# Last head of the latent attention: query weights in four free places, gates of its own, latent queries and a page turn between its products, rotary chunk first; scores of tile 4 as 320 + 320

## What is computed

```python
q = jnp.einsum('bsc,chd->bshd', cq, w_qb)
q_nope, q_rope = q[..., :QK_NOPE], q[..., QK_NOPE:]
...
k_nope = jnp.einsum('bsc,chn->bshn', ckv, w_uk)
v = jnp.einsum('bsc,chv->bshv', ckv, w_uv)
...
sc = (jnp.einsum('bqhn,bkhn->bhqk', qn_b, k_nope)
      + jnp.einsum('bqhr,bkr->bhqk', qr_b, kpe)).astype(jnp.float32) * MLA_SCALE
sc = jnp.where(kpos[None, :] <= qpos[:, None], sc, NEG_INF)
p = jax.nn.softmax(sc, axis=-1).astype(v.dtype)
return jnp.einsum('bhqk,bkhv->bqhv', p, v)
...
# samples: the query goes into the latent, and the paged latents are keys and values
q_lat = jnp.einsum('bthn,chn->bthc', q_nope, w_uk)
s_past = (jnp.einsum('bthc,bsc->bhts', q_lat, past_ckv)
          + jnp.einsum('bthr,bsr->bhts', q_rope, past_kpe)).astype(jnp.float32) * MLA_SCALE
...
h <- h + RMSNorm_post( W_o( attn(RMSNorm_pre(h)) * silu(gate) ) )
```

## Time and profile before

| | us |
|---|---|
| median of 3 runs | 1676.52 |
| the profiled execution, its time | 1678.97 |
| its span, first to last instruction | 1677.3 |
| busy: TensorE matmul / weight load | 1583.8 / 1484.5 |
| busy: VectorE / ScalarE / GpSimd | 825.3 / 547.3 / 736.8 |
| mean granted TensorE clock | 0.987 |

### The profile page before, as it was taken

How to read it: one execution, slowest core, us unless ns; L and a number is a source line. 1 busy time by engine, 2 the same in 40 slices (tenths; PEclk the granted TensorE clock), 3 DMA queues, 4 the chain that set the end, 5 groups by cost and what they waited for, 6 DMA issues and landing times.

```text
span 1677.3 us, 28038 instructions
## 1 busy us (share of the span) xinstructions
PE 1583.8 (94%) x10778; PEld 1484.5 (89%) x10778; DVE 825.3 (49%) x1459; ACT 547.3 (33%) x1203; POOL 736.8 (44%) x891
## 2 busy tenths in 40 slices
PE   7999999899999999999998888999899999988997
PEld 7999999799999898999997557999799999966796
DVE  5137311676675757575665430006873421178426
ACT  4113101344444444444443320012231311277322
POOL 2432323154655545455545512546522324278720
PEclk9999999999999999999999999999999999999998
DMA  4112232021111211112117977227254323354223
GB/s 179 60 52 100 85 123 99 19 63 55 64 57 56 70 55 60 48 61 66 64 39 257 330 284 271 64 75 239 99 216 151 106 76 132 102 154 121 76 79 149
DMA packets 101406, 186.92 MB, mean 111 GB/s; under 512 B 11058, under 2 KB 65091, under 8 KB 100995
## 3 DMA queue, kind: packets, MB, share of 16 engines
q1 hardware_dynamic: 86628, 139.36, 24.9%
q0 software_dynamic: 8448, 24.65, 4.2%
q10 hardware_dynamic: 6208, 21.26, 3.2%
HBM read 137.42 MB, written 49.89 MB: 112 GB/s over the span
## 4 chain that ended last, share of the span: by engine, by line
PE 80%; DVE 8%; ACT 5%; issue 3%; DMA 2%; POOL 1%; SPq 1%; DVEq 0%; ACTq 0%; POOLq 0%
PE ps L128 26%; PE ps L928 8%; PE ps L2123 6%; PE ps L994 6%; PE ps L2331 5%; PE ps L978 4%; ACT s_prob L2603 3%; PE ps L934 3%; PE ps L941 2%; PE ps L958 2%; PE ps L959 2%; PE ps L962 2%; PE ps L960 2%; PE ps L961 2%; PE ps L2257 2%
## 5 line engine op out<-in xcount | busy, mean ns | idle before, releaser
L654 POOL TENSOR_SCALAR b_prob<-b_prob,b_share 128x896 f32<-128x896 f32 (+7 forms) x128 | 97.4, 762 | 194.5 <-DVE b_share L856 192.6
L1779 POOL CAST w_hi_d<-w_raw_d 128x1024 fp32r<-128x1024 f32 x38 | 42.3, 1113 | 225.0 <-PE ps L128 109.4
L128 PE MATMUL ps<-a_xh,w_hi_a 128*128 128x344 f32 x552 | 119.5, 325 | 11.0 <-DVE a_xl L397 11.0
L755 ACT ACTIVATE b_pth<-ps 128x512 fp32r<-128x512 f32 (+1 forms) x160 | 86.2, 554 | 104.9 <-PE ps L978 95.4
L128 PE MATMUL ps<-a_xl,w_hi_a 128*128 128x344 f32 x552 | 118.4, 323 | 0.0
L128 PE MATMUL ps<-a_xh,w_lo_a 128*128 128x344 f32 x552 | 118.1, 323 | 0.0
L746 ACT ACTIVATE b_prob<-ps,b_least 128x896 f32<-128x896 f32 (+7 forms) x128 | 94.8, 743 | 58.1 <-DVE b_least L847 57.1
L847 DVE TENSOR_REDUCE b_least<-ps 128x1 f32<-128x896 f32 (+7 forms) x128 | 96.1, 751 | 33.3 <-PE ps L964 32.5
L861 DVE TENSOR_TENSOR b_ptl<-ps,b_pth 128x512 fp32r<-128x512 f32 (+1 forms) x160 | 99.0, 631 | 27.0 <-ACT b_pth L755 26.0
L128 PEld LDWEIGHTS ps<-a_xh,w_hi_a 128*128 128x128 f32 x552 | 94.1, 191 | 12.0 <-issue 11.5
L106 POOL CAST w_hi_a<-w_raw_a 128x1024 fp32r<-128x1024 f32 x23 | 23.9, 1040 | 175.6 <-PE ps L128 171.4
(11 more groups left out here) (356 smaller groups left out, 4586.8 us busy)
## 6 DMA issues: line engine op xcount, KB each, us to landing
w_raw_d<-in_w_tiles SPq DMA_DIRECT2D x46, 512.0 KB, 3.5
c_pages<-in_cache_pages SPq DMA_DIRECT2D x80, 160.0 KB, 4.8
w_raw_a<-in_w_tiles SPq DMA_DIRECT2D x23, 512.0 KB, 3.5
gate_scratch<-a_stage ACTq DMA_DIRECT2D x16, 512.0 KB, 2.6
b_gate<-gate_scratch SPq DMA_DIRECT2D x64, 128.0 KB, 2.6
oh_scratch<-b_oh POOLq DMA_DIRECT2D x64, 128.0 KB, 2.1
ol_scratch<-b_ol POOLq DMA_DIRECT2D x64, 128.0 KB, 2.1
xo_h<-oh_scratch SPq DMA_DIRECT2D x16, 512.0 KB, 11.3
```

What stands on the lines that cost most here:

```text
L128: mm = nc.tensor.matmul(ps[:, bank + c, 0:CH], wt, xt[:, k0 + k, c * CH:(c + 1) * CH], start=first and x == 0, stop=last and x == 2)
L654: nc.gpsimd.tensor_scalar(prob[:, n % 4, 0:keys], prob[:, n % 4, 0:keys], share[:, n % 4:n % 4 + 1], 1.0, ALU.mult, ALU.mult).then_inc(nor ...
L755: nc.scalar.activation(pth[:, n % 4, 0:cols], ps[:, 4 + n % 2, 0:cols], ACT.Copy).then_inc(pt_hi, 1)
```

## The change

1. **Tile 4's scores**: 640 keys as 320 in each of two banks, before 512 + 128. Maximum and exponent read 2 x 320.
2. **Rotary chunk first**, at the end of head 14: `job("qr", 7, 1)` takes the place of `job("qn", 15, 1)`, which moves to the end, behind tile 1's scores and group 1's mixing. ScalarE and VectorE are put in a matching order; the four sine products are cut in two pairs.
3. **Last head**: each engine gets a `last(h)` in place of `odd(15)`. On TensorE the latent queries stand in two halves of 8 heads inside it (now bank 7), and page turn (0, 0, 0) in front of group 1's mixing. On GpSimd the norm of tile 3 stands in front of the cuts of groups 0 and 2.
4. **Query weights** in four tiles of 512 KB, in places that head 15 does not use (weights of even units, values of an older head), loaded by SP once head 13 is mixed. The loads stand in front of the page numbers' lookup.
5. **Gates of head 15** in a tile of their own (`b_last_gate`), loaded once tile 3 of head 14 is scored.
6. Rows of latent queries (`c_q_rows`) lie in the heads' keys, both halves kept by ScalarE inside head 15; round 1's pages also wait for the query transposes.

```diff
@@ tensor, score
+            wide = 320 if t == 4 else 512
             for b in range(t // 4 + 1):
-                keys = slice(b * 512, min((t + 1) * P, (b + 1) * 512))
+                keys = slice(b * wide, min((t + 1) * P, (b + 1) * wide))
@@ tensor, even
-            job("qn", h + 1, 1), turn(h, 1, 1), mix(h, 2, 1), mix(h, 2, 2), job("qr", p, 1), mix(h, 1, 0), mix(h, 1, 1)
-            job("k", h + 2, 0), score(h + 1, 1)
+            if h < H - 2:
...
+            else:
+                job("qr", p, 1), turn(h, 1, 1), mix(h, 2, 1), mix(h, 2, 2), score(h + 1, 1), mix(h, 1, 0), mix(h, 1, 1)
+                job("qn", h + 1, 1)
@@ tensor, new
+        def last(h):
+            turn(h, 3, 0), turn(h, 3, 1), score(h, 4)
+            bank_read(len(JOBS) - 1)
+            samples.latent_queries(pe, 0)
+            turn(h, 3, 2), score(h, 5), turn(h, 3, 3), mix(h, 3, 0), mix(h, 3, 1), turn(h, 0, 0)
+            mix(h, 3, 2), mix(h, 3, 3), score(h, 2), turn(h, 2, 0), turn(h, 2, 1), mix(h, 0, 0), score(h, 3)
+            turn(h, 2, 2), mix(h, 2, 0)
+            samples.latent_queries(pe, 1)
+            mix(h, 2, 1), mix(h, 2, 2), turn(h, 1, 0), turn(h, 1, 1)
+            pe.wait_ge(exped, tile_no(h, 2) + 1)
+            samples.first_turn(pe)
+            mix(h, 1, 0), mix(h, 1, 1)
@@ vector, even, last head ahead
+                first_products(p, 1), last_products(p, 1, range(2)), turned_low(h, 1, 1), apply_gate(h, 2)
+                invert(h + 1, 0), last_products(p, 1, range(2, 4)), greatest(h + 1, 1), rope_sum(p, 1)
+                apply_gate(h, 1), rope_low(p, 1), low("qn", h + 1, 1)
@@ gpsimd, new
+        def last(h):
+            norm(h, 1), norm(h, 4), norm(h, 5), cut(h, 3), norm(h, 2), norm(h, 3), cut(h, 0), cut(h, 2)
@@ scalar, new
+        def last(h):
+            turned_high(h, 3, 0), turned_high(h, 3, 1)
+            samples.keep_queries(act, 0)
+            turned_high(h, 3, 2), turned_high(h, 3, 3), exponents(h, 4), exponents(h, 5), turned_high(h, 0, 0)
+            exponents(h, 2), turned_high(h, 2, 0), turned_high(h, 2, 1), turned_high(h, 2, 2), exponents(h, 3)
+            samples.keep_queries(act, 1)
+            turned_high(h, 1, 0), turned_high(h, 1, 1)
@@ sync
             if h == H - 1:
-                find_pages(sp)
+                sp.wait_ge(pj_done, JOB_NO[("v", H // 2 - 1, 3)] + 1)
+                sp.wait_ge(mixed, chunk_no(H - 3, 1, 1) + 1)
+                samples.load_query_weights(sp)
+                samples.find_pages(sp)
@@ sync, load_gate
+            if h == H - 1:
+                sp.wait_ge(scored, tile_no(H - 2, TILE_ORDER[-1]) + 1)
+                sp.wait_ge(gate_in[n % 4], 16 * (n // 4))
-            if due(n - 3):
+            elif due(n - 3):
                 sp.wait_ge(gated, n - 3)
@@ samples, tensor
-        turn(0, 0, 0), turn(0, 0, 1)
+        turn(0, 0, 1)
         heads.all_done(pe)
-        pe.wait_ge(q_act, 1)
-        pe.wait_ge(q_dve, 1)
+        pe.wait_ge(q_rows_kept, 2)
```

More of the change, by code:

```diff
@@ L785, in scalar @@
         for h in range(0, H, 2):
-            even(h), odd(h + 1)
+            even(h)
+            odd(h + 1) if h < H - 2 else last(h + 1)
     def vector(dve):
@@ L819, in rope_products, with last_products @@
             nc.vector.tensor_tensor(rot[:, 0, :], ps[:, bank, 0:CH], g.cos[:, cols], ALU.mult).then_inc(qr_mul, 1)
-            for r in range(4):
+        def last_products(p, c, parts):
+            if ("qr", p, c) not in JOB_NO:
+                return
+            bank, cols = job_bank(JOB_NO[("qr", p, c)]), slice(c * CH, (c + 1) * CH)
+            for r in parts:
                 to, src = slice(32 * r, 32 * r + 32), slice(32 * (r ^ 1), 32 * (r ^ 1) + 32)
@@ L1059 @@
 HG = H // 4
-WK_CHUNK = 3
 LOW_PARTS = (range(0, 4), range(4, 8), range(8, 12), range(12, 16))
@@ L1135, in load_pages, with load_query_weights @@
                           ).then_inc(page_in[by_pool][r * CHUNKS + c], 16)
+    def load_query_weights(sp):
+        for i, part in enumerate(g.wk):
+            nc.sync.dma_start(part[:], a["w_uk_turned"][4 * i:4 * i + 4].rearrange("h p k -> p h k")).then_inc(wk_in, 16)
     def load_low(part):
@@ new lines, in latent_queries @@
+    def latent_queries(pe, half):
+        if half == 0:
+            pe.wait_ge(wk_in, 16 * len(g.wk))
+            pe.wait_ge(g.qs_kept, H)
+        else:
+            pe.wait_ge(q_rows_kept, 1)
+        for u in range(2 * half, 2 * half + 2):
+            for e in range(HG):
+                mm = nc.tensor.matmul(ps[e * QPAD:(e + 1) * QPAD, 7, u % 2 * KVL:(u % 2 + 1) * KVL],
+                                      g.qs_nope[:, u * HG:(u + 1) * HG, :].rearrange("p h b -> p (h b)"), g.wk[u][:, e, :],
+                                      start=True, stop=True)
+        mm.then_inc(q_made, 1)
@@ new lines, in kept, with turn_rows @@
+    def kept(pe, n):
+        pe.wait_ge(act_kept if n % 2 == 0 else dve_kept, n // 2 + 1)
+    def turn_rows(pe, r, c, s):
+        n = item(r, c, s)
+        by_pool = pool_share[r * CHUNKS + c]
+        if s == 0:
+            pe.wait_ge(page_in[0][r * CHUNKS + c], 16 * 4 * (QUAD - len(by_pool)))
+        if s == 2 and by_pool:
+            pe.wait_ge(page_in[1][r * CHUNKS + c], 16 * 4 * len(by_pool))
+        if n >= 2:
+            kept(pe, n - 2)
+        for f in range(2):
+            for k in range(4):
+                mm = nc.tensor.transpose(ps[:, 2 * (n % 2) + f, k * P:(k + 1) * P],
+                                         pages[r][:, 4 * c + k, s, f * P:(f + 1) * P], g.ident[:])
+        mm.then_inc(rows_turned, 1)
```

153 lines of the change are left out of this document (83 added, 70 removed).

## The result

| | before | after |
|---|---|---|
| median of the runs, us | 1676.52 | 1667.82 (5 runs, 1664.03 to 1670.08) |
| the profiled execution, us | 1678.97 | 1667.97 |
| its span, us | 1677.3 | 1666.3 |
| busy: TensorE matmul / weight load, us | 1583.8 / 1484.5 | 1579.0 / 1482.8 |
| busy: VectorE / ScalarE / GpSimd, us | 825.3 / 547.3 / 736.8 | 823.6 / 548.2 / 738.0 |

The ratio of the changed kernel to the one before is 0.9941 (0.9927 to 0.9954): faster, by 7.7 to 12.2 us. Forecast were 1665.9 us and a range of 1662.5 to 1669.9; measured were 1667.8, a gain of 8.7 where 10.6 was forecast.

What follows compares the result with a forecast made beforehand. TensorE was taken as the full engine in the heads (busy 194.6 of 200 us). Terms 3.8 + 3.3 + 4.1 - 0.6 = 10.6 us took the median from 1676.52 to 1665.9 us, range 1662.5 to 1669.9.

Steps and rivals of the forecast that it cites:

- Tile 4: Tile 4's scores in heads 0 to 14: ten 320-column matmuls save 0.25 us a head, 3.8 us in all.
- Rotary swap: End of head 14: rotary product first, so head 15's tile 4 starts 1.4 us earlier and runs faster; 3.3 us together.
- the gate's wait: End of head 14: TensorE, with tile 1's scores in front, waits some 0.3 us for head 14's gate.
- Rest of the last head: After tile 4's scores to the query transposes: 5.4 us lost, less 0.3 new waits and 1.0 for ScalarE's wait; 4.1 us.
- the wait for ScalarE: Page turn behind the last head: ScalarE waits for GpSimd's clearing to place the sample queries; this wait grows by 1.0 us.
- The norm is late because GpSimd first splits group 0: Last head: the split and its two stores, 2.65 us, delay tile 3's norm; the change puts the norm in front.
- The overlap at the stage's end: End of sample stage: up to four pages overlap the heads' outputs transfer, between 0 and -1.7 us; -0.6 taken.
- GpSimd's row: Rival: GpSimd's row of work sets the sample stage, so the gain is 8.5 us, 1668.0; chance 0.10.
- only 0.7 of slack: Sample stage: GpSimd's page loads had 2.8 us of slack, which becomes 0.7, so no wait, just.
- softmax chain: Rival: the last head's softmax chain keeps its length, moved work only fills holes; gain 8.2 us, 1668.3; chance 0.10.

Runs made afterwards that it cites:

- Experiment 9: The kernel before with only GpSimd's order changed, tile 3's norm ahead of group 0's split in head 15; ratio 1.0007 (0.9994 to 1.002).
- experiment 4: The changed kernel with GpSimd splitting group 0 of the last head ahead of tile 3's norm, as before the change; ratio 0.9922 of the kernel before.
- experiment 5: The changed kernel with both halves of the latent queries behind the last mixing, the page turn still inside; ratio 0.9937 of the kernel before.
- experiment 12: The changed kernel with four page loads of the fourth chunk moved from GpSimd to SP; ratio 0.9952 of the kernel before.
- Experiment 6: The changed kernel with TensorE's wait for the heads' outputs split in two parts; ratio 0.9944 of the kernel before.
- 10: The changed kernel with group 0's split ahead of tile 3's norm and the outputs' wait in two parts; ratio 0.9927, median 1665.12 us.
- 7: The changed kernel with GpSimd clearing the sample queries' place before it splits group 2 of the last head; ratio 0.9948 of the kernel before.
- 2: The changed kernel with tile 4's scores back at 512 + 128; ratio 0.9947 of the kernel before.
- the control: The changed kernel again, unaltered, timed beside the experiments; ratio 0.9945 (0.9929 to 0.9962) of the kernel before.
- 1: The kernel before with tile 4's scores as 320 + 320 and nothing else of the change; ratio 0.9970 (0.9958 to 0.9983).
- 3: The changed kernel with the rotary swap undone and tile 1's scores behind the mixing again; ratio 0.9950 of the kernel before.
- 11: The changed kernel with group 0's split ahead of the norm and the latent queries behind the last mixing; ratio 0.9947 of the kernel before.

## Why the prediction was right, and where it was not

1. **Tile 4**, forecast -3.8 in 15 heads, 0.25 each: measured 0.246 in the changed kernel, 0.25 alone, 4.1 +- 1.1 in the times. Right, in mechanism and size.
2. **Rotary swap**, forecast -3.3 as 1.4 + 1.9: the start of head 15's tile 4 came 1.42 earlier (39.19 - 37.52 less the 0.25), and it took 1.71 less. The wait is 0.23 for 0.3, the gate's wait 0.33 for 0.3. Undoing it costs 2.9 in the trace. (The two products started 3.62 apart, not 3.5, which changes nothing.) Right.
3. **Rest of the last head**, forecast -4.1 as 5.4 - 0.3 - 1.0. From the end of tile 4's scores to the end of the query transposes TensorE now takes 19.5 (888.92 to 908.41). The 24.35 of the forecast takes its start from one view and its end from another; with both from the timeline (897.30 to 921.50) it is 24.2. So it is 4.7 less where 5.1 was forecast, ahead of the wait for ScalarE. That wait was forecast to grow by 1.0 and grew by 0.3, from 0.33 to the 0.61 in front of the page turn at 910.93. The size is right.

   **The step that failed is the one under it**: "The norm is late because GpSimd first splits group 0 ... the change puts the norm of tile 3 in front". In the kernel before, the split held the norm up for 1.1 of the 2.40: the reciprocal that it needs was ready at 909.22 and it started at 910.36. Experiment 9 takes the split away there, and TensorE still waits 1.35 for that norm.

   In the changed last head its place is worth nothing: experiment 4 puts the split back in front, and not 0.1 us of the head's length returns; experiment 5 takes the latent queries out, and the wait doesn't return either. What is left of the change there is TensorE's order and VectorE's (the gate of group 0 and tile 3's maximum earlier). TensorE had nothing between group 2's first mixing and the turn of tile 3 (908.44 to 911.12); now it has the second half of the latent queries (900.71, 1.0) and twelve more matmuls of group 2's mixing (901.71 to 903.16, 1.45), and in experiment 5 the twelve alone cover the norm. VectorE, before, at the gate of group 0, the maximum and the reciprocal of tile 3, and after:

```profile
907.21 0.42 DVE L872 TENSOR_TENSOR b_ov<-ps,b_gate 128x256 f32<-128x256 f32 x1
907.54 0.68 DVE L847 TENSOR_REDUCE b_least<-ps 128x1 f32<-128x512 f32 x1
909.06 0.16 DVE L856 RECIPROCAL b_share<-b_total 128x1 f32<-128x1 f32 x1 [0.84 <-ACT b_prob L746]
```

```profile
898.38 0.42 DVE L924 TENSOR_TENSOR b_ov<-ps,b_last_gate 128x256 f32<-128x256 f32 x1
899.65 0.69 DVE L900 TENSOR_REDUCE b_least<-ps 128x1 f32<-128x512 f32 x1 [0.24 <-PE ps L1029]
```

Before, the gate came right in front of the maximum, so the split of group 0 couldn't start ahead of 907.69; now the gate starts 1.27 ahead of the maximum, and the split fits in front of the norm but for 0.7. That TensorE's new order is what removes the rest of the 2.40 is read from these rows; it was not tried in the kernel before, and how much each of the two orders carries stays open.

4. **The overlap at the stage's end**, forecast -0.6 of 0 to -1.7: nothing. First mixing to first output matmul is 31.38 and 31.36, with idle 2.79 and 2.76.
5. **GpSimd's row**, a rival with 0.10 ("only 0.7 of slack"): in the changed kernel it is true in part, and two of the forecast's own signs of it are there: page turns that wait for a page, and the sample queries that wait for the clearing by over 1 us (2.42). Page waits are 1.5 and 2.9 in two traces; the stretch from the query transposes to the first mixing grew by 0.5 and 2.7 where the forecast had 1.0. In the traces with the transposes 20.3 to 20.6 behind tile 4 (experiment 12, with other page loads, left out), the waits go with the place of GpSimd's first page load behind tile 4's start: 0.2 to 0.7 where it is at 24.7 to 25.3 (experiments 4, 6 and 10), 1.5 at 25.7, 2.0 at 26.0 (7), 2.4 and 2.9 at 26.4 (2 and the control). The forecast's own numbers put it at 25.05 (922.8 - 5.3 - 892.45). The slack of 0.7 was worked out from page loads alone; the row's length also hangs on how soon the store lands that frees the split's buffer (0.34 and 1.05 of wait), and on the 1.91 that the norm waits at the head of it.
6. **Not foreseen**: the 1.45 at 1.2 GHz behind the outputs' transfer.

In the trace of the changed kernel, the first score came 1.75 earlier for no reason of the change. Without that, the first low part of the outputs stands 9.4 earlier, against 10.6 forecast and 9.0 at equal clock. In the control's trace it is 7.2 earlier, and the 2.2 between the two traces are at the page turns. Of the missing 1.2 the clock's 1.45 is more than all. The last head is 0.6 short of its terms (6.4 less where 1.9 + 5.1 was forecast) and the first half of head 0 0.2; 0.5 less at the page turns and 0.6 of overlap that didn't come make up for these. So the time was right because the terms were near, and the explanation of one of them was for the greater part wrong. The number alone doesn't tell: 1667.8 lies nearer to the 1668.0 of the rival "GpSimd's row" and the 1668.3 of "softmax chain" than to the forecast's 1665.9, and the range took in both.

## What to carry to other kernels

Where a wait is ascribed to the instruction queued in front of its releaser, ask when that instruction's own input was ready: here the split was queued in front of the norm, but the norm's own input was ready only 1.1 before the norm started, so the split accounted for 1.1 of a wait of 2.40. With TensorE's and VectorE's new orders around it, it accounted for nothing. When TensorE is pulled forward by several us, walk the whole row of the engine that issues its next loads, buffers and landing stores included, since it is the next to bind. And of two splits of one product over banks, take the even one if the short piece's matmuls start further apart than their columns ask for.

## What was not expected of the hardware

The same idle of TensorE, 2.74 to 2.92 us in front of the same 24 matmuls, was followed by 1.00 in the three traces of kernels with the old last head (before, 1 and 9) and by a stretch at 0.50 in all eight with a new one (the changed kernel, its control, 2, 3, 4, 7, 11 and 12), where 12 matmuls took 3.39 to 3.78 for 2.12. The 31 us in front are the same work in all of them. Experiment 6 took the idle away and the stretch with it, so the idle is a condition; what else decides, the runs don't show. In experiment 5 this idle was only 1.07, with 1.00 behind it, and the clock had fallen already behind an idle of 1.36, which was harmless in the kernel before (a wait in front of the same 16 matmuls, there in 1.92, here in 3.36):

```profile
978.35 3.36 PE L1484 MATMUL ps<-c_turned,c_q_b 128*32 128x512 f32 x16 [1.36 <-issue]
```

The page "TensorE: Matmul & The Clock Gate" of the Trainium skill (section "What's actually happening") says that the number of slow matmuls at the start of one kernel differs from run to run (6, 11 or 14). No run here counts those; what is seen here is the mean clock of whole executions, and it varies within one kernel too: the control's six executions fall into three at 1665.2 to 1665.9 and three at 1669.8 to 1672.1, with mean clocks of 0.989 to 0.990 and 0.984 to 0.985.
